# Taking two turned units of a weight group together: sixteen wide products, then sixteen narrow ones

## The reference, cut to what matters

```python
qkv = h @ w_qkv                       # 2048 -> 6144
x = x + y @ w_o                       # 2048 -> 2048
g = causal_dwconv(h @ w_gate)         # 2048 -> 5632, three taps over the tokens
u = h @ w_up
x = x + (silu(g) * u) @ w_down        # 5632 -> 2048
# second block, after its two attentions and a cross attention:
x = x + square(relu(hm @ w_up_2)) @ w_down_2   # 2048 -> 8192 -> 2048
```

## Time and profile before

| | us |
|---|---|
| median of three runs | 2410.36 (2410.36 to 2411.93) |
| the profiled execution | 2412.81 |
| its span, first to last instruction | 2411.0 |
| TensorE matmul busy | 2385.6 (99%) |
| VectorE busy | 1567.6 (65%) |
| ScalarE busy | 1245.3 (52%) |
| mean granted TensorE clock | 0.998 of full |

### The profile page before, as it was taken

How to read it: one execution, slowest core, us unless ns; L and a number is a source line. 1 busy time by engine, 2 the same in 40 slices (tenths; PEclk the granted TensorE clock), 3 DMA queues, 4 the chain that set the end, 5 groups by cost and what they waited for, 6 DMA issues and landing times.

```text
span 2411.0 us, 32038 instructions
## 1 busy us (share of the span) xinstructions
PE 2385.6 (99%) x12314; PEld 2018.5 (84%) x12314; DVE 1567.6 (65%) x2447; ACT 1245.3 (52%) x1955; POOL 5.2 (0%) x12
## 2 busy tenths in 40 slices
PE   8999999999999999999999999999999999999998
PEld 7888877888888888888887878887888888888887
DVE  5786777777777657755668545664766557556555
ACT  5566556655555435544656555655544444444443
POOL 0000000000000000000000000000000000000000
PEclk9999999999999999999999999999999999999999
DMA  6544344555555665465564544554565665666664
GB/s 236 185 156 161 129 157 148 164 195 176 208 177 184 207 192 184 175 227 191 166 204 148 176 131 134 189 184 123 175 195 189 193 191 183 200 183 195 210 193 153
DMA packets 119783, 432.13 MB, mean 179 GB/s; under 512 B 13472, under 2 KB 13744, under 8 KB 119120
## 3 DMA queue, kind: packets, MB, share of 16 engines
q1 hardware_dynamic: 118080, 424.10, 54.8%
q0 software_dynamic: 976, 5.39, 0.6%
q10 hardware_dynamic: 576, 0.60, 0.1%
HBM read 427.93 MB, written 2.11 MB: 178 GB/s over the span
## 4 chain that ended last, share of the span: by engine, by line
PE 95%; DVE 2%; ACT 1%; issue 1%; DMA 0%; SPq 0%; DVEq 0%; ACTq 0%
PE bank L475 29%; PE bank L481 15%; PE bank L461 15%; PE bank L463 15%; PE bank L462 15%; PE bank L693 1%; PE bank L520 1%; DVE lo_w L1325 1%; DVE xT L1468 1%; PE bank L677 0%; DMA raw_w<-in_w_qk 0%; PE bank L564 0%; PE bank L645 0%; PE bank L654 0%; PE bank L602 0%
## 5 line engine op out<-in xcount | busy, mean ns | idle before, releaser
L1325 DVE TENSOR_TENSOR lo_w<-raw_w,hi_w 128x1024 fp32r<-128x1024 f32 x804 | 965.2, 1218 | 601.5 <-ACT hi_w L884 600.9
L884 ACT ACTIVATE hi_w<-raw_w 128x1024 fp32r<-128x1024 f32 x804 | 832.2, 1052 | 581.1 <-PE bank L463 396.8
L475 PE MATMUL bank<-xT,hi_w 128*128 128x512 f32 x3008 | 758.1, 394 | 0.6 <-DVE xT L1468 0.6
L475 PEld LDWEIGHTS bank<-xT,hi_w 128*128 128x128 f32 x3008 | 542.6, 189 | 99.1 <-issue 1.3
L481 PEld LDWEIGHTS bank<-xT,lo_w 128*128 128x128 f32 x3008 | 410.3, 190 | 29.5
L481 PE MATMUL bank<-xT,lo_w 128*128 128x256 f32 x3008 | 419.3, 282 | 0.0
L461 PE MATMUL bank<-hi_w,act_hi 128*128 128x512 f32 x864 | 336.4, 389 | 0.0
L462 PE MATMUL bank<-lo_w,act_hi 128*128 128x512 f32 x864 | 336.2, 389 | 0.0
L463 PE MATMUL bank<-hi_w,act_lo 128*128 128x512 f32 x864 | 336.1, 389 | 0.0
L461 PE MATMUL bank<-hi_w,xT 128*128 128x512 f32 (+1 forms) x736 | 294.5, 400 | 2.2 <-DVE xT L1468 2.1
L463 PE MATMUL bank<-hi_w,xT 128*128 128x512 f32 (+1 forms) x736 | 286.9, 390 | 0.0
(11 more groups left out here) (315 smaller groups left out, 1549.8 us busy)
## 6 DMA issues: line engine op xcount, KB each, us to landing
raw_w<-in_w_up SPq DMA_DIRECT2D x216, 512.0 KB, 4.2
raw_w<-in_w_down SPq DMA_DIRECT2D x216, 512.0 KB, 4.1
raw_w<-in_w_gate SPq DMA_DIRECT2D x88, 512.0 KB, 4.0
raw_w<-in_w_in SPq DMA_DIRECT2D x72, 512.0 KB, 3.6
raw_w<-in_w_qk SPq DMA_DIRECT2D x64, 512.0 KB, 3.6
raw_w<-in_w_v SPq DMA_DIRECT2D x32, 512.0 KB, 4.0
raw_w<-in_w_o SPq DMA_DIRECT2D x32, 512.0 KB, 3.5
raw_w<-in_w_out SPq DMA_DIRECT2D x32, 512.0 KB, 3.6
```

Of the source, the lines that this page charges most:

```text
L475: e.matmul(pair[c][:, :], hi_w[:, slot, at:at + P], both[:, kt].rearrange("p h t -> p (h t)"), start=(kt == 0), stop=False, skip_group_che ...
L884: e.activation(hi_w[:, u % SPLIT_SLOTS, 0:unit_cols[u]], raw_w[:, u % RAW_SLOTS, 0:unit_cols[u]], ACT.Copy).then_inc(s["w_hi"], 1)
L1325: e.tensor_tensor(lo, raw_w[:, u % RAW_SLOTS, 0:unit_cols[u]], hi.bitcast(F32), ALU.subtract).then_inc(s["w_lo"], 1)
```

## The change

TensorE's program takes two units of a turned group together, when both lie in the same call of `units(n)` and in the same group: the wide products of both, then the narrow products of both. It waits for `w_hi` of the second unit before that unit's wide products, and for `w_lo` of each unit before its narrow ones. `w_used` is still signalled after a unit's narrow products. The other engines' programs stay as they are.

```diff
-            def turned_products(u):
+            def high_products(u):
+
+                g, pair, slot = groups[group_of[u]], group_banks(group_of[u]), u % SPLIT_SLOTS
+                both = turned_in(g.stage)
+                e.wait_ge(s["w_hi"], u + 1)
+                if g.fresh:
+                    input_landed(g, u)
                 for c in range(2):
...
+            def low_products(u):
...
                 e.wait_ge(s["w_lo"], u + 1)
                 for c in range(2):
...
                     last.then_inc(s["w_used"], 1)
 
             def units(n):
-                for u in range(done[0], done[0] + n):
+                u, end = done[0], done[0] + n
+                while u < end:
                     g = groups[group_of[u]]
-                    e.wait_ge(s["w_hi" if g.kind == "turned" else "w_lo"], u + 1)
...
+                    if g.kind == "turned":
+                        run = 2 if u + 1 < end and u < g.last else 1
+                        for v in range(u, u + run):
+                            high_products(v)
+                        for v in range(u, u + run):
+                            low_products(v)
+                        u += run
+                        continue
+                    e.wait_ge(s["w_lo"], u + 1)
                     if g.fresh:
                         input_landed(g, u)
-                    if g.kind == "turned":
-                        turned_products(u)
-                        continue
```

More of the change, by code:

```diff
@@ L465, in product @@
                 last.then_inc(s["w_used"], 1)
-            def turned_products(u):
-                g, pair = groups[group_of[u]], group_banks(group_of[u])
-                both, slot = turned_in(g.stage), u % SPLIT_SLOTS
-                kts = [(u - g.first) * g.per + k for k in range(g.per)]
+            def high_products(u):
[4 more added lines that the diff above has]
+                    input_landed(g, u)
                 for c in range(2):
-                    for k, kt in enumerate(kts):
-                        at = k * TURNED_COLS + c * P
+                    for k in range(g.per):
+                        kt, at = (u - g.first) * g.per + k, k * TURNED_COLS + c * P
                         e.matmul(pair[c][:, :], hi_w[:, slot, at:at + P], both[:, kt].rearrange("p h t -> p (h t)"),
                                  start=(kt == 0), stop=False, skip_group_check=True)
+            def low_products(u):
+                g, pair, slot = groups[group_of[u]], group_banks(group_of[u]), u % SPLIT_SLOTS
+                both = turned_in(g.stage)
                 e.wait_ge(s["w_lo"], u + 1)
                 for c in range(2):
-                    for k, kt in enumerate(kts):
-                        at = k * TURNED_COLS + c * P
+                    for k in range(g.per):
+                        kt, at = (u - g.first) * g.per + k, k * TURNED_COLS + c * P
                         last = e.matmul(pair[c][:, 0:TOK], lo_w[:, slot, at:at + P], both[:, kt, 0, :],
@@ L491, in units @@
                         e.wait_ge(s[name], count)
+                    if g.kind == "turned":
[7 more added lines that the diff above has]
+                    e.wait_ge(s["w_lo"], u + 1)
                     if g.fresh:
                         input_landed(g, u)
-                    if g.kind == "turned":
-                        turned_products(u)
-                        continue
                     for c in range(2):
                         product(u, c)
-                done[0] += n
+                    u += 1
+                done[0] = end
             def last_units(n):
```

## The result

| | median us | profiled span us |
|---|---|---|
| before | 2411.14 (2410.36 to 2411.97, 4 runs) | 2411.0 |
| changed | 2428.79 (2428.54 to 2431.01, 4 runs) | 2426.7 |

The changed kernel takes 1.0077 times as long, interval 1.0065 to 1.0089: 17.7 us more, where 16.4 were forecast. Of the four executions before, two took 2410.36 us and two some 2411.95; against the two short ones the changed kernel's short ones (2428.5 to 2429.0) take 18.2 us more.

A forecast was written before the change was run, and what follows sets the result against it. TensorE, busy 2385.6 of 2411.0 us, was taken as the bound. Pauses of + 20.0 us less 3.6 us of switches gave + 16.4 us on the median 2410.36: 2427 us, range 2418 to 2437.

The forecast's parts named there:

- The slip: Gate drain: unit 330's slot released 1.84 us later, so the drain and unit 335's rounding come 1.39 us late.
- E: Start of the up1 group (units 332 to 335) behind a gate group (328 to 331); 1015.50 in the trace before.
- The early want: A pair's second unit needs its rounded weights 0.95 us earlier; alone this leaves 0.5 us in up1, no wait.
- The count: One TensorE pause of 0.95 us per up1 group with the small margin: 21 pauses, 20.0 us; none in up2.
- The switches: TensorE: each of 179 pairs has one narrow-to-wide switch less, 0.02 us each, 3.6 us gained.
- The qk stretch: Up to the first output projection, ScalarE waits for TensorE to free slots; cost put at zero, 2 us at most.
- The clock: Rival: each pause in up1 lowers TensorE's granted clock, 71 us more, 2498 us; chance 0.03.
- The covered drains: Up1 and up2 drains slip but keep 1.6 us margin; rival that they run out: 15 us more, 2442 us, chance 0.05.
- the faster rival: TensorE pairs give over 27 ns each with no pause, faster by 0.2%; 2403 us at 40 ns; chance 0.02.

The follow-up runs named there:

- e3: Changed kernel with VectorE's rest moved from ahead of the gate drain to just before the drain's last product; 2410.49 us, 1.0002 of the kernel before.
- e6: e3 with ScalarE's copy of the first tile's half also put ahead of the rounding; 2408.63 us, 0.9990 of the kernel before.
- e1: Changed kernel with only the last pair of each gate group taken apart again; 2408.99 us, 0.9995 of the kernel before.
- e2: Changed kernel with only the last pair of each up1 group taken apart; 2409.05 us, 0.9997 of the kernel before.
- e5: Changed kernel edited to take units singly, every second unit of a group narrow products first; 2406.89 us, 0.9985 of the kernel before.
- e4: Changed kernel with up to four units of a group taken together instead of two; 2530.32 us, 1.0501 of the kernel before.
- e7: Changed kernel with all four units taken together in up1 groups only, pairs elsewhere; 2489.92 us, 1.0332 of the kernel before.

## Why the prediction was right

*The slip.* The chain was forecast against E and can be read against E: unit 334's rounding at - 0.69 (measured - 0.70), its rest at + 0.40 (+ 0.40), the drain's first VectorE step at + 1.53 (+ 1.54), unit 335's rounding at + 7.13 (+ 7.13), the load at + 8.24 (+ 8.23). e3 and e6 show that it is a matter of order on the two engines.
The Trainium skill's page "TensorE: Matmul & The Clock Gate", section "Architectural detail: the array is 16× 32×32, not 1× 128×128", says that ScalarE's and VectorE's queues are strictly first in, first out. The trace agrees: the copy that L1353 needs was written by E + 0.63, and it still started at E + 1.54, behind the rest.

*The early want.* 0.95 us, and alone harmless (e1), as the step said. The pause needs both parts (e2).

*The count.* 21 pauses, none in up2 and none in the first up1 group, as matched from the roundings before.

*The switches.* 0.02 us per pair was read from two timelines; blocks of sixteen take 3.66 and 1.91 us as forecast, and e1, e2, e5 and e6, in which no up1 load waits, lie 1.3 to 3.6 us below the kernel before. Only for e5 (and barely e6) is the interval clear of 1. The form N/2.4 + 2.5 ns, which the prediction holds against its rows, is called the gap of an isolated product by that section of the Trainium skill's page "TensorE: Matmul & The Clock Gate", "Back-to-back issue gap"; for a stream with weight loads the section gives about 131 ns at 512 columns. The trace agrees with neither: 227 ns.

*What was sized a little off.* The qk stretch was put at zero with 2 us as its bound, because ScalarE waits there for TensorE. It costs 1.3 us net, in a single wait for tanh: the same slip of 1.39 us, met by a product that had less to spare. These 1.3 us already hold the gain of the stretch's 26 pairs (0.5 us), which the forecast counted apart. So the sum is 16.4 + 0.5 + 1.3 = 18.2 us, what the short executions show. That the forecast missed the difference of the medians by only 1.3 us and not by 1.8 is luck, since the median before is that of two short and two longer executions.

*A slip of reading.* The drain has five steps on ScalarE (two of L905, two of L911, one of L915 in the kernel before), not seven. Nothing in the sum hangs on it.

*The rivals.* The clock does not fall behind pauses of 0.95 us: its mean in the changed kernel is 0.999. e4 and e7 show that the rival was real, with a pause three times as long. Its price was too high: the fall in cross attention cost 2.4 us by the matched units, not 3.4, and one in e7 1.54. The Trainium skill's page "TensorE: Matmul & The Clock Gate", section "A second HAM failure mode: psum-queue depth-cycling", tells of idles frequent enough to let the clock swing and gives no length for them. The 21 pauses of 0.95 us, one in some 23 us, did not do it here. The covered drains of up1 and up2 held with their margin in pairs, and ran out with four units together (70 waits in e4). No run shows a pair worth the 0.027 us that the faster rival needed: blocks stay at 0.02.

## What to carry to other kernels

When two steps are merged on one engine, write down two shifts for every buffer: how much earlier the second input is wanted and how much later the first is released, and put both against the smallest margin that the trace has, not the mean one. Follow a later release through the queue it stands in: here a rounding for a unit nobody needed for 6 us held up a drain that another unit needed. If the merge is wanted for the dense run itself, look for an order that has the run without the late release: mirroring every second unit gave the whole gain of the runs and was the fastest kernel here (2406.89 us).

## What the runs showed of the hardware that was not expected

A product of 512 columns takes 0.227 us behind others of its kind, and eight of them behind narrow ones take 0.02 us more. Start to start in the kernel before (up2), the first five behind narrow ones take 233, 236, 228, 232 and 231 ns, and the last ones 227. Why is not shown. Of 21 pauses of one length, about 2.9 us, 13 were followed by a stretch at half clock (1.2 GHz) and 8 were not, in one and the same execution (e7); the 21 pauses of 0.95 us in the changed kernel never were. In cross attention the kernel before had such a fall and the changed one did not, with pauses of about the same sum, which moves a profiled span by 2.4 us and must be set aside before two traces are subtracted.
